# Hybrid attention and mixture-of-experts trunk on one core: first modulation group moved ahead, last extra tile in halves, combination put off by one block

## What is computed

```python
def trunk_layer(x, c, pos, past, ...):
    mod = jax.nn.silu(c) @ w_ada_l + b_ada_l
    sh1, sc1, gt1, sh2, sc2, gt2 = [m_[:, None, :] for m_ in jnp.split(mod, 6, axis=-1)]
    h = rms_norm(x, g_mix_l) * (1.0 + sc1) + sh1
    mix, new_rows = mixer_block(h, pos, past, w_in_l, w_pa_l, w_pb_l, w_out_l)
    x = x + gt1 * mix
    h = rms_norm(x, g_ffn_l) * (1.0 + sc2) + sh2
    x = x + gt2 * hier_moe(h, w_rg_l, b_rg_l, w_re_l, b_re_l, w_eg_l, w_eu_l, w_ed_l)
    return x, new_rows
...
    merged = jax.nn.sigmoid(ga) * (ya @ w_pa_l) + jax.nn.sigmoid(gb) * (yb @ w_pb_l)
    return merged @ w_out_l, new_rows
...
        hdn = jax.nn.silu(xb @ w_eg[e]) * (xb @ w_eu[e])
        return hdn @ w_ed[e]
```

## Time and profile before

| what | value |
|---|---|
| runs of the kernel | 1053.59, 1043.97, 1046.73 us; median 1046.73 |
| profiled execution | 1046.63 us, its span 1044.8 us |
| PE busy | 951.1 us (91%), 7692 instructions |
| weight load on PE | 593.5 us (57%) |
| DVE, ACT, POOL busy | 378.5, 293.0, 71.9 us |
| moved by DMA | 320.02 MB, mean 306 GB/s |
| mean granted clock of TensorE | 0.98 of full speed |
| ring tiles | 272 of 1024 KB, median 15.9 us from issue to landing |

### The profile page before, as it was taken

One profiled execution on the slowest core, in us unless ns is written; L12 is line 12 of the kernel. 1 busy time (PEld: TensorE's weight loads), 2 busy tenths in 40 slices (PEclk: granted clock), 3 DMA queues, 4 the chain that ended last, 5 costly groups with the idle time before them and its releaser, 6 DMA issues.

```text
span 1044.8 us, 22182 instructions
## 1 busy us (share of the span) xinstructions
PE 951.1 (91%) x7692; PEld 593.5 (57%) x7693; DVE 378.5 (36%) x1073; ACT 293.0 (28%) x683; POOL 71.9 (7%) x146
## 2 busy tenths in 40 slices
PE   5899999999999987889999999998999899788996
PEld 2567777467855443434556776755786545344443
DVE  2227732223261332223343484132326133232334
ACT  2334664410032111101144466552013211111112
POOL 1112000000100000000002110000010000000000
PEclk9899999999999999989999999999999999999998
DMA  9996323899387999999989333179952499999992
GB/s 365 321 388 239 121 87 117 345 421 420 128 321 290 422 422 422 421 395 410 422 300 421 128 120 121 61 274 421 421 230 111 147 417 422 422 421 408 404 422 105
DMA packets 66445, 320.02 MB, mean 306 GB/s; under 512 B 6170, under 2 KB 28130, under 8 KB 29378
## 3 DMA queue, kind: packets, MB, share of 16 engines
q1 hardware_dynamic: 63552, 314.86, 75.4%
q10 hardware_dynamic: 2690, 3.70, 1.1%
q0 software_dynamic: 128, 0.40, 0.1%
HBM read 316.42 MB, written 2.52 MB: 305 GB/s over the span
## 4 chain that ended last, share of the span: by engine, by line
PE 68%; DMA 17%; DVE 5%; ACT 5%; issue 3%; SPq 1%; POOLq 0%; POOL 0%; ACTq 0%; DVEq 0%; PEldq 0%
PE ps L618 21%; DMA ring<-wstream 17%; PE ps L1121 8%; PE ps L704 8%; PE ps L1096 5%; PE ps L1109 4%; PE ps L1130 4%; PE ps L1033 3%; PE ps L1099 3%; PE ps L772 1%; ACT work L1340 1%; PE ps L656 1%; DVE work L1536 1%; DVE top L1535 1%; PE ps L938 1%
## 5 line engine op out<-in xcount | busy, mean ns | idle before, releaser
L618 PE MATMUL ps<-h,ring 128*128 128x288 f32 x512 | 131.2, 409 | 1.0 <-ACT work L1257 1.0
L1121 PE MATMUL ps<-ring,h 128*32 128x512 f32 x896 | 114.0, 617 | 18.9 <-DMA ring<-wstream 15.9
L618 PE MATMUL ps<-work,ring 128*128 128x288 f32 x512 | 128.2, 409 | 0.0
L618 PEld LDWEIGHTS ps<-h,ring 128*128 128x128 f32 x512 | 94.9, 190 | 29.1 <-issue 4.4
L618 PEld LDWEIGHTS ps<-work,ring 128*128 128x128 f32 x512 | 96.0, 190 | 25.4
L704 PE MATMUL ps<-h,ring 128*128 128x288 f32 x416 | 105.1, 412 | 1.9 <-DVE h L1505 1.9
L1412 ACT ACTIVATE mraw<-ps 128x512 f32<-128x512 f32 x64 | 38.2, 597 | 239.7 <-PE ps L1121 239.3
L1771 DVE SCALAR_TENSOR_TENSOR h<-pads,rms,h 128x288 f32<-128x288 f32 x128 | 60.7, 516 | 93.2 <-issue 93.2
L704 PEld LDWEIGHTS ps<-h,ring 128*128 128x128 f32 x416 | 79.3, 192 | 26.4 <-issue 4.5
L1130 PEld LDWEIGHTS ps<-fold,mraw 128*128 128x128 f32 x512 | 62.1, 191 | 52.1 <-ACT mraw L1412 47.7
L1130 PE MATMUL ps<-fold,mraw 128*128 128x32 f32 x512 | 69.0, 278 | 21.7 <-PE ps L1109 18.3
(11 more groups left out here) (249 smaller groups left out, 970.2 us busy)
## 6 DMA issues: line engine op xcount, KB each, us to landing
ring<-wstream SPq DMA_DIRECT2D x272, 1024.0 KB, 15.9
work<-wstream SPq DMA_DIRECT2D x16, 1024.0 KB, 20.9
work<-pages SPq DMA_DIRECT2D x32, 192.0 KB, 3.2
work<-pages SPq DMA_DIRECT2D x32, 128.0 KB, 2.2
x<-x_in SPq DMA_DIRECT2D x1, 1152.0 KB, 5.3
out_y<-h ACTq DMA_DIRECT2D x4, 288.0 KB, 2.1
cs<-consts SPq DMA_DIRECT2D x1, 834.0 KB, 26.4
h<-rows_of_tokens ACTq DMA_DIRECT2D x2, 288.0 KB, 3.2
```

The lines of the kernel that those rows point to most:

```text
L618: last = mm(out, w[:, (k0 + k) * stride:(k0 + k) * stride + 128], rhs(k), start=(k == 0), stop=(k == n - 1))
L1121: last = mm(pgu[32 * c:32 * c + 32, :], xs[:, k, :], w[:, c * 512:(c + 1) * 512], start=(k < 4), stop=(k >= 4), skip_group_check=True)
```

## The change

Five edits. (1) The first modulation group stands as the fifth job between the attention units, ahead of `g4`, and its tiles stand behind the first two gate tiles in the stream; all later gate jobs move by one place. (2) The eighth extra tile is loaded in two halves, the first as soon as the gathers from the near half of `hrow` are done (`far`), which now lies apart from the other half. (3) In all expert loops a block's combination comes one block later, between up and down of the block after the next up; the first combination of a layer adds a zeroed `comb` (cleared by DVE), and a second one stands ahead of the layer's last down. (4) The wait for `y_done` and the slots' release stand behind turn. (5) `keep_warm(1)` behind the sums of squares is gone.

```diff
@@ -85,7 +85,7 @@
-BETWEEN = [[f"g{n}"] for n in range(16)] + [["mod1"], ["mt1"], ["mod2"], [], ["mt2"], []]
+BETWEEN = [[f"g{n}"] for n in range(4)] + [["mod1"]] + [[f"g{n}"] for n in range(4, 16)] + [["mt1"], ["mod2"], [], ["mt2"], []]
@@ -130,7 +130,8 @@
 def stream(l):
-    dense = [(l, pair) for pair in range(P_QI, P_EXP)]
+    order = [*range(P_QI, P_GATE + 2), *range(P_MOD1, P_MOD2), *range(P_GATE + 2, P_MOD1), *range(P_MOD2, P_EXP)]
+    dense = [(l, pair) for pair in order]
     if l == 0:
@@ -299,7 +300,7 @@
         hs4 = carve(7168, KD, 128)
-        hrow = carve(4864, 2, D)
+        hrow = carve(4864, 2, 2, 512)
         hrow_s = yb[:, :]
@@ -443,6 +444,10 @@
+            def load_half(of, j, i):
+                part = slice(i * PAIR // 2, (i + 1) * PAIR // 2)
+                sp.dma_start(extra[j][:, part], wstream[of * PAIRS + P_EXP + APART[j], :, part]).then_inc(extra_w[j], 16)
+
             first_expert = {AT[l, P_EXP]: l for l in range(DEPTH)}
@@ -461,8 +466,10 @@
                     load_extra(of, 6)
+                    far.wait(sp, of)
+                    load_half(of, 7, 0)
                     banks.wait_full(sp, of, f"x{KD - 1}.1")
-                    load_extra(of, 7)
+                    load_half(of, 7, 1)
                 if i == KD + 1:
@@ -1030,7 +1037,7 @@
                         for c in range(4):
-                            mm(outs[c][:, 0:T], hrow[:, tb, (k0 + c) * 128:(k0 + c + 1) * 128], sel[:, tb, part],
+                            mm(outs[c][:, 0:T], hrow[:, k0 // FAR, tb, c * 128:(c + 1) * 128], sel[:, tb, part],
                                start=(tb == 0), stop=False, skip_group_check=True)
@@ -1081,7 +1088,7 @@
                     if j in APART:
-                        pe.wait_ge(extra_w[APART.index(j)], 16 * (l + 1))
+                        pe.wait_ge(extra_w[APART.index(j)], 16 * (l + 1) * (1 + (APART.index(j) == EXTRA - 1)))
                         return extra[APART.index(j)]
@@ -1089,8 +1096,8 @@
-                    pe.wait_ge(y_kept, n + 1)
-                    pe.wait_ge(comb_ready, n + 1)
+                    pe.wait_ge(y_kept, n + l + 1)
+                    pe.wait_ge(comb_ready, n + l + 1)
                     for i in range(2):
@@ -1130,12 +1137,6 @@
-                def turn_and_combine(n):
-
-                    turn(n)
-                    combine(n)
-                    pe.reg_add(seen, seen, 1)
-
                 def look_ahead(next_blocks):
@@ -1148,13 +1149,14 @@
                     turn(pe.snap(seen, min_val=0, max_val=200))
-                    pe.sem_inc(combined, 1)
                     pe.reg_add(seen, seen, 1)
                             n = up(0)
+                            combine(n)
                             down(n, 0)
-                            turn_and_combine(n)
+                            turn(n)
+                            pe.reg_add(seen, seen, 1)
                     pe.wait_ge(gu_done, pe.snap(seen, min_val=0, max_val=200) + 1)
@@ -1163,16 +1165,21 @@
                     more = look_ahead(next_blocks)
+                    combine(n)
                     down(n, e - 1, rounds)
                         with pe.Fori(1, more) as b:
-                            turn_and_combine(pe.snap(seen, min_val=0, max_val=200))
-                            down(up(e, rounds), e, rounds)
+                            turn(pe.snap(seen, min_val=0, max_val=200))
+                            pe.reg_add(seen, seen, 1)
+                            n = up(e, rounds)
+                            combine(n)
+                            down(n, e, rounds)
+                    turn(pe.snap(seen, min_val=0, max_val=200))
                     held = [j for j in range(3 * e - 1, 3 * e + 2) if j not in APART]
                         pe.sem_inc(w_free, len(held))
-                    turn_and_combine(pe.snap(seen, min_val=0, max_val=200))
+                    pe.reg_add(seen, seen, 1)
@@ -1186,10 +1193,11 @@
                 total = pe.snap(seen, min_val=1, max_val=200)
+                combine(total)
                 down(total, N_EXP - 1)
                 pe.sem_inc(w_free, 1)
-                combine(total, True)
+                combine(pe.snap(total + 1, min_val=1, max_val=201), True)
@@ -1215,7 +1223,6 @@
                 ss.up(last)
-                keep_warm(1)
                 if l + 1 < DEPTH:
@@ -1371,7 +1378,7 @@
                     banks.wait_full(a, l, f"h{n}")
-                    banks.done(act(hrow[:, tb, (n % 2) * 512:(n % 2 + 1) * 512], banks.ap(l, f"h{n}"), ACT.Copy,
+                    banks.done(act(hrow[:, n % 2, tb, :], banks.ap(l, f"h{n}"), ACT.Copy,
                                    scale=dest[:, 15, tb:tb + 1]), l, f"h{n}")
@@ -1760,13 +1767,15 @@
                 banks.wait_full(d, l, f"x{KD - 1}.1")
+                V.memset(comb, 0.0).then_inc(comb_ready, 1)
+                d.sem_inc(y_kept, 1)
                 hold(d, seen)
                         at = d.snap(e * MAXBLK + b, min_val=0, max_val=N_EXP * MAXBLK - 1)
-                        d.wait_ge(comb_ready, n + 1)
+                        d.wait_ge(comb_ready, n + l + 2)
                         for i in range(2):
```

## The result

The changed kernel took 1054.3 us (median of 21 runs, 1050.7 to 1060.0), the kernel before, run beside it, 1051.3 us (21 runs, 1044.0 to 1058.0). The ratio is 1.0035, 95% interval 1.0019 to 1.0052: 3.7 us slower. This ratio is the figure to hold against the forecast of +0.3%. The profiled execution of the changed kernel was one of its longest: 1059.66 us, span 1057.9, which is 13 us above the profiled one of before. Most of these 13 us are the scatter between executions, so I read places in the two traces and take sizes from the experiments.

What follows compares the result with a forecast made beforehand. The prediction took the expert loops to be fed at the DMA's rate, both layers ending within half a microsecond of it. Terms -3.5 + 0 + 6.9 - 0.3 = +3.1 on 1046.6 gave 1049.7, rounded to 1050 us; range 1044.5 to 1057.0.

Steps and rivals of the forecast that it cites:

- The modulation group: End of attention: PE's waits for the second group's tiles go, 2.55 us in layer 0 and 0.99 in layer 1, -3.5.
- The half tile: Eighth extra tile, ahead of the ring's first request: loading half earlier gains 0, at best 1.25 us a layer.
- The combination put off: Expert loops: later slot release and one more combination a layer cost 2.7 us in layer 0, 4.2 in layer 1, +6.9.
- The end: Behind each layer's last up: three combinations instead of two, 1.64 - 0.37 = +1.3 us a layer.
- The dips: DMA runs dry longer behind the first two slots (+0.5 layer 0, +2.0 layer 1) and at expert 20 (+0.9 each).
- Release with down's end or with turn: Slots freed 1.64 us later if with down's end (taken), 2.4 if once turn is dispatched, making +6.9 into +9.7.
- The 0.37 us per block: Blocks that free slots: moving down's wait behind turn saves PE 0.37 us, only lengthening its later waits for tiles.
- The warming matmul: Layer ends: without it the next matmuls begin some 0.4 us earlier; -0.3 taken, ends -0.6 and +1.4.
- A: Rival: the DMA dips cost nothing, only the end's +2.6 stays, 1045.4 us; chance 0.20.
- B: Rival: PE sets the loop's pace, so 0.37 us a block counts, 1025.7 us; chance 0.05.
- D: Rival: the second modulation group still waits for its tiles, +3.5 on the sum, 1053.2 us; chance 0.06.
- C: Rival: one more code pause ahead of expert 20's release, 3.9 us a layer, 1057.5 us; chance 0.11.

Runs made afterwards that it cites:

- comb_only: Kernel before with only the combination put off by one block and the wait for down's end and release behind turn: ratio 1.0079, +8.3 us.
- after_warm: Changed kernel with the warming matmul put back: ratio to before 1.0036 (1.0017 to 1.0056).
- after_early_free: Changed kernel with the wait for down's end and the release back between down and turn, combination still put off: ratio to before 1.0047.
- free_behind_turn: Kernel before with only the wait for down's end and the release moved behind turn, combination unmoved: ratio 0.9983, -1.8 us.
- mod_half: Kernel before with the modulation group moved and the eighth extra tile in halves: ratio 0.9969 (0.9949 to 0.9988).
- after_no_comb: Changed kernel with combination, counts, wait and release taken back to before's; group, half tile and missing warming matmul stay: ratio to before 0.9997.
- warm_only: Kernel before with only the warming matmul left out: ratio 1.0055 (1.0034 to 1.0076), +5.8 us.
- mod_only: Kernel before with only the modulation group behind the fourth gate job and its tiles earlier in the stream: ratio 0.9960, -4.2 us.
- pad_more: Kernel before, warming matmul kept, four register instructions added behind it in each layer, counted as one more instruction a layer: ratio 1.0003 (0.9981 to 1.0026).

## Why the prediction was right in its sum and wrong in one step

**Time.** +0.3% was predicted, +0.35% (0.19 to 0.52) measured.

**The modulation group, -3.5.** Right: -4.2 us alone, and the waits of 2.55 and 0.99 us are gone from the trace. The pages move later with the units, as said.

**The half tile, 0.** Right within +- 2.8 us. No finer statement is to be had.

**The combination put off, +6.9.** Right in size: +8.3 us alone, 7.0 and 4.0 us as differences in company (each within 2.6 to 2.9 us), 5.6 us by the loops of the profiles. Its steps one by one:
- The end, +1.3 a layer: last tile's use to the end of the last combination is 1030.89 - 1022.51 = 8.38 us before (layer 1) and 9.96 after (layer 0), +1.6. Mechanism and size right; 0.23 us of it is a wait of the third down for DVE that I had not seen.
- The dips, 1.4 and 2.9 us a layer: where expert 31's second tile was waited for, it came 195.7 us behind the ring's request (mean of ten landings in the first eight kernels of the table, 192.4 to 197.8) and 197.1 us with the put-off combination (four landings in comb_only, after_warm and the changed kernel, 196.4 to 198.0), +1.4 a layer against a mean of 2.2 that the two dips of a layer were to cost (few landings, and the two ranges overlap). By place I was off: in the changed kernel's profile the two dips of layer 0 lost 2.8 and 3.6 us more where I had 0.5 and 0.9, with a slow first up step and a pause ahead of the releases; layer 1's start lost 2.1 where I had 2.0, and expert 20 had no dip there where I had 0.9. That dips do not add, because a stream already behind has slots waiting, fits this and was not tested.
- Release with down's end or with turn: by the times my choice held. SP issues 0.15 to 0.16 us behind down's end both at comb_only's expert 20 (462.64, 462.79) and in the changed kernel's first block of layer 0 (335.26, 335.42), the 0.15 that I took. What I had not seen is that a pause between down and turn now delays the release too, by 1.84 us at expert 20 of layer 0. In after_early_free it came 0.75 us behind down's end there (459.95, 460.70) instead of 2.04; its last tile landed at 195.3 and 196.4 us, 1.3 us earlier on average, and its time was no better.
- "The 0.37 us per block only shortens stretches in which PE then waits longer for tiles" is right in the list of waits (13 become 31 or 34) and not quite right in time: free_behind_turn gained 1.8 us (interval -0.2 to +3.7), with 203.4 and 202.0 us in the loops of the two kernels that have it. If the gain is real, a DMA limit does not make PE's time quite worthless. That PE falls behind at each pause and a shorter block catches up sooner would explain it; no run shows it.

**The warming matmul, -0.3.** The step that failed: that the matmuls behind it only begin "some 0.4 us earlier" without it, with the slow clock as an upper end of +1.4. The slow clock is what came each time, and it costs more. Timeline behind the last sums with the matmul (mod_half; last row: busy time by stretch, clock third from the right):

```profile
535.88 1.12 PE L634 MATMUL ps<-cs 128*128 128x512 f32 x2
536.65 0.60 DVE L1472 RECIPROCAL rms<-rms 128x72 f32<-128x72 f32 x1 [0.40 <-ACT rms L1258]
537.31 1.11 PE L1231 MATMUL ps<-rms,cs 128*128 128x72 f32 x8 [0.30 <-DVE rms L1472]
538.26 1.93 PE L634 MATMUL ps<-cs 128*128 128x512 f32 x4
540.06 2.21 PE L711 MATMUL ps<-h,ring 128*128 128x288 f32 x7
...
537.30:540.00 2.70, 2.69 (x12) 1.57 (x12) 1.43 (x4) 0.51 (x1) 0.00 (x0) 1.00 0.78 214
```

and without it (after_no_comb; first row: the end of the sums, by stretch):

```profile
533.00:534.00 1.00, 1.00 (x40) 0.90 (x37) 0.41 (x2) 0.53 (x2) 0.00 (x0) 0.50 1.22 300
...
534.87 0.60 DVE L1471 RECIPROCAL rms<-rms 128x72 f32<-128x72 f32 x1 [0.39 <-ACT rms L1257]
535.53 1.98 PE L1230 MATMUL ps<-rms,cs 128*128 128x72 f32 x8 [1.36 <-DVE rms L1471]
537.30 3.71 PE L634 MATMUL ps<-cs 128*128 128x512 f32 x4
540.81 2.40 PE L711 MATMUL ps<-h,ring 128*128 128x288 f32 x7
...
535.50:540.80 5.30, 5.27 (x12) 3.22 (x13) 3.15 (x9) 1.99 (x5) 0.00 (x0) 0.50 0.68 192
```

In this pair the spread of the roots begins 0.06 us behind the reciprocal's end both times: the matmul does not delay it. In before it did, because the warming matmul itself ran at the lower clock:

```profile
535.92 2.08 PE L627 MATMUL ps<-cs 128*128 128x512 f32 x2
...
535.92:536.90 0.98, 0.98 (x4) 0.50 (x2) 0.45 (x2) 0.26 (x1) 0.00 (x0) 0.50 1.03 267
```

That was no single case. Of the 18 layer ends with the matmul, it ran for 1.68 to 2.08 us in 12, and the spread then began 0.15 to 0.51 us behind the reciprocal; in the other 6 it took 1.12 us and delayed nothing. So up to 0.45 us of gain were there to be had, as I said. The price is what I had wrong. Without the matmul the spread took 1.98 us in all ten ends, at clock 0.50, the lower of the two levels, and in layer 0 the first projection came 4.5 to 5.3 us behind the spread's start; with it the spread took 1.01 to 1.82 us and the projection came 2.65 to 3.8 us behind. The pause of 1.36 us is not always what lowers the clock: in after_no_comb it was at 0.50 already during the sums, in after_early_free it was 1.00 there and 0.50 behind the pause. The matmul either keeps the clock up or, where it has fallen, has it back at 1.00 by the spread or soon behind.

Over all profiles, without the matmul layer 0's end is 2.0 us longer and layer 1's 0.5, so +2.5, beyond the end of +1.4 that I gave. The timed differences are 5.8, 3.5, 2.9 and -0.1 us (each within 2.2 to 3.5 us), mean 3.0. The Trainium skill (TensorE: Matmul & The Clock Gate, Part 1: The HAM clock gate) gives TensorE 1.2 GHz when it has been idle and 2.4 GHz when busy; the granted 0.50 and 1.00 agree with these two levels.

**Why the sum came out all the same.** With the group as timed and the other terms as the profiles give them, -3.7 (the group: -4.2 us alone, -3.2 as the difference of the two kernels with the release behind turn) + 0 + 5.6 + 2.5 = +4.4 us, within the measured 2.0 to 5.5. The missing 2.8 us at the warming matmul stood beside a combination taken 1.3 us too dear; that the sum still hit is in part luck. What stays open is why comb_only and warm_only, timed alone, cost 8.3 and 5.8 us, and the sum of the four is 7 us too high. Their intervals, taken as independent, leave +- 4.9 us on that sum, and somewhat more since all four are held against the same runs of before; chance alone hardly covers the gap, and that the parts act on each other stays possible. In warm_only's profile the excess is in layer 1's loop (209.8 us), with 7.2 us of pauses; that the pauses were it in all its 12 runs was not shown.

**The rivals.** A is refuted by comb_only, B by all. D is refuted by the trace. C, one more pause a layer, did not come as a rule: the pauses sum to 8.2 to 12.9 us with the put-off combination (mean 11.1) and 8.9 to 14.5 in the first eight kernels (mean 11.2). In layer 0 a pause did stand ahead of expert 20's release, as C said, in the changed kernel (1.84 us) and in after_warm (1.55), not in comb_only. And their places changed, from the middle of layer 1's loop to its start (5.4 of 6.8 us), in all four kernels with the new loop.

**What would show it.** Block 5.51 us (said: 5.4), 7.5 us at DMA pace, three combinations behind the last up, deeper dips at three of the four places: seen. I had also said that the prediction is wrong if pauses come or go. They did, from 8.9 to 12.9 us in this pair of profiles; with 8.2 to 14.5 us over all 14 that sign could not tell anything. "More blocks with waits" was a bad test: after_early_free has the later DMA with 13 waits, free_behind_turn has 34 without it.

## What to carry to other kernels

When a loop is fed at the DMA's rate, a step put ahead of the release of a slot makes the DMA late where it has run dry (here the last tile landed 1.4 us later a layer), and an extra round of a put-off step costs nearly its full time behind the last tile (1.6 us a layer); together they were worked out from rows of before to within 2 us. Move the wait, not the work: moving the wait for down's end behind an independent step gave the whole gain of the block (5.75 to 5.36 us), and the reordering only cost, though only 1.8 us (interval -0.2 to 3.7) of it reached the kernel's time. A matmul without use in a wait of 1.4 us was not idle work here; before one is removed, read the durations of the matmuls behind it, and its own, in several executions, since they come at either clock.

## What the runs showed that was not expected

- The first up step behind the start of the expert loop runs at the lower clock or not by the execution: in layer 0 it took 1.92 to 1.93 us in four of 14 profiles and 3.0 to 3.6 in the other ten, behind much the same wait of 1.1 to 1.4 us. The two steps from 62 us on (L716, L772) took 1.20 and 7.17 us in seven of 14 profiles and 2.0 to 2.2 and 7.6 to 9.1 us in the other seven, behind the same pause of 1.4 us. One pair of profiles shows such differences where the change has none: before against mod_only loses 2.9 us near 62 us, which hides the group's whole gain in layer 0.
- Pauses without releaser move with code that is not in the loop: two of 4.3 us in before, four of 7.2 us in warm_only, whose loop is the same; and they also move between kernels whose code ahead of them is the same (in layer 0: 0.93 us at the combination in before, 2.04 in warm_only, both near 455). The Trainium skill (Runtime: NRT & Kernel Launch, Instruction fetch mechanics) gives a fetch behind a taken branch as a cause of such stalls; no row names the cause here, and pad_more, which moves the code by one instruction a layer, showed no cost within its interval of +- 2.4 us.
